# Sample attention with each key page on 32 partitions, turned by VectorE in 32 x 32 blocks, and scored by 32 x 32 tiles of TensorE

## The reference

```python
past_k = cache_fox_k[page_table].reshape(db, past_len, H_F, D_F)
past_v = cache_fox_v[page_table].reshape(db, past_len, H_F, D_F)
...
s = jnp.einsum('bqhd,bkhd->bhqk', qi, k, preferred_element_type=F32) * scale
s = s + ci.astype(F32).transpose(0, 2, 1)[..., None] - ckT
...
p = jax.nn.softmax(s, axis=-1)
return jnp.einsum('bhqk,bkhd->bqhd', p.astype(v.dtype), v)
...
mix = (g[:, :, 0] * ret_out + g[:, :, 1] * fox_out + g[:, :, 2] * mem_out) @ w_out
```

## Time and profile before

| | us |
|---|---|
| median of three runs | 3666.53 (3665.11 to 3673.05) |
| profiled execution, its own time | 3673.46 |
| its span, first to last instruction | 3671.6 |
| `phase_sample` in the span | about 2092 to 2616 |
| of it, 7 of the 8 sequences (56 of 64 quads) | 2130 to 2560 |

### The profile page before, as it was taken

The page is one execution under the profiler, slowest core; times in us unless marked ns, Lnnn a source line. Parts: engine busy times, 40 slices in busy tenths (PEclk is TensorE's granted clock), DMA queues, the critical chain, the costliest instruction groups (busy, mean ns, idle before and its releaser), DMA issues. The chain is left out here.

```text
span 3671.6 us, 56105 instructions
## 1 busy us (share of the span) xinstructions
PE 3314.7 (90%) x21121; PEld 2999.5 (82%) x21121; DVE 888.4 (24%) x1581; ACT 625.5 (17%) x1163; POOL 794.6 (22%) x696
## 2 busy tenths in 40 slices
PE   5999999997988898786799899999796999999996
PEld 5999999996887798554688666666686999999995
DVE  2111111114206211555101022222314111111114
ACT  3000000002101100344000144434203000000003
POOL 0232222323120131022111111111021223233220
PEclk8999999998997899899899999999798999999998
DMA  5111111111110112210211299999311111111111
GB/s 141 35 51 40 42 49 34 49 49 29 29 44 22 41 40 67 91 48 17 52 43 43 60 297 307 300 305 303 121 29 29 34 46 50 33 51 43 37 37 55
DMA packets 328667, 293.12 MB, mean 80 GB/s; under 512 B 33640, under 2 KB 249064, under 8 KB 328048
## 3 DMA queue, kind: packets, MB, share of 16 engines
q1 hardware_dynamic: 317136, 275.93, 24.3%
q0 software_dynamic: 11424, 15.76, 1.6%
HBM read 279.34 MB, written 12.26 MB: 79 GB/s over the span
## 5 line engine op out<-in xcount | busy, mean ns | idle before, releaser
L207 PE MATMUL f_acc<-x_hi,w_hi_last 128*128 128x364 f32 x1056 | 233.5, 329 | 27.5 <-SPq L489 27.5
L165 POOL CAST w_hi_first<-w_raw_first 128x1024 fp32r<-128x1024 f32 (+1 forms) x96 | 82.9, 863 | 738.4 <-issue 301.3
L207 PE MATMUL f_acc<-x_hi,w_hi_first 128*128 128x364 f32 x1056 | 233.5, 329 | 6.9 <-SPq L489 6.9
L207 PE MATMUL f_acc<-x_lo,w_hi_last 128*128 128x364 f32 x1056 | 234.0, 330 | 0.0
L207 PE MATMUL f_acc<-x_hi,w_lo_last 128*128 128x364 f32 x1056 | 234.0, 330 | 0.0
L207 PE MATMUL f_acc<-x_hi,w_lo_first 128*128 128x364 f32 x1056 | 233.9, 330 | 0.0
L207 PE MATMUL f_acc<-x_lo,w_hi_first 128*128 128x364 f32 x1056 | 233.7, 329 | 0.0
L207 PEld LDWEIGHTS f_acc<-x_hi,w_hi_last 128*128 128x128 f32 x1056 | 184.0, 189 | 28.0 <-issue 28.0
L165 POOL CAST w_hi_last<-w_raw_last 128x1024 fp32r<-128x1024 f32 (+2 forms) x92 | 73.5, 799 | 614.2 <-PE f_acc L207 610.2
L596 DVE SCALAR_TENSOR_TENSOR br<-f_acc,br 128x1092 f32 x88 | 114.1, 1296 | 368.8 <-PE f_acc L207 368.8
L207 PEld LDWEIGHTS f_acc<-x_hi,w_hi_first 128*128 128x128 f32 x1056 | 184.0, 189 | 7.1 <-issue 7.1
(11 more groups left out here) (399 smaller groups left out, 6321.8 us busy)
## 6 DMA issues: line engine op xcount, KB each, us to landing
br<-cache_fox_k SPq DMA_DIRECT2D x256, 256.0 KB, 5.6
br<-cache_fox_v SPq DMA_DIRECT2D x256, 256.0 KB, 6.5
w_raw_first<-w_ffn_gate SPq DMA_DIRECT2D x22, 512.0 KB, 3.8
w_raw_first<-w_ffn_up SPq DMA_DIRECT2D x22, 512.0 KB, 3.8
w_raw_last<-w_ffn_gate SPq DMA_DIRECT2D x22, 512.0 KB, 3.8
w_raw_last<-w_ffn_up SPq DMA_DIRECT2D x22, 512.0 KB, 3.8
w_raw_first<-w_ffn_down SPq DMA_DIRECT2D x40, 256.0 KB, 2.9
w_raw_last<-w_ffn_down SPq DMA_DIRECT2D x40, 256.0 KB, 2.8
```

The lines of the kernel that those rows point to most:

```text
L165: self.nc.gpsimd.tensor_copy(hi, raw).then_inc(self.high[s], 1)
L207: mm = self.nc.tensor.matmul(out[:, b, 0:width], w[s][:, k, :], x[:, k, b * width:(b + 1) * width], start=(k == 0 and first), stop=(k == k ...
```

## The change

Each key page is loaded onto 32 partitions (page x of a quad onto partitions 32x to 32x + 31, four tokens of 2 KB on each), by a DMA of its own as before. VectorE then turns blocks of 32 x 32 from `k_in` to `d_kt` in SBUF, two instructions of 128 x 1024 for a quad; TensorE's 16 transposes, the four ScalarE copies and their PSUM buffers are gone. The scores of a quad are 64 matmuls with 32 rows and 32 columns of the array and 128 columns of keys each, over all 16 positions of the array; each row group writes a PSUM bank of its own. The queries stand for this in `d_q_rep`, built by ScalarE for each sequence in 18 small copies, two in each step.

A score row is now a query of a head for all pages: the tile of a step is 128 x 512 (it was 128 x 256), there are four transposes of weights (two before), 16 products of 128 columns (8 of 256), and the exchange between pairs of rows is gone. ScalarE, no longer VectorE, copies the turned weights out. Scores, turned weights and products have one PSUM buffer each (two before). The filler is in all 9 steps, in blocks of 364, 364 and 296 + 64 tokens.

The bias ring now lies in `mem_kt` and `mem_v`. A slot holds two quads (four before), comes by 4 DMAs of 16 partitions, and there are 4 slots per sequence. The page table comes by one DMA (two before).

```diff
-        kt = [[g.mem_kt[:].rearrange("p a k -> p (a k)").rearrange("p (x c k) -> p x c k", x=2, c=PAIRS),
...
-        ring = [g.sb(ctx, f"d_ring{x}", [P, QUAD, 2, P]) for x in range(2)]
+        kt = [g.sb(ctx, f"d_kt{x}", [P, QUAD, H_F * DF]) for x in range(2)]
+        ring = [x[:].rearrange("p a k -> p (a k)").rearrange("p (m k) -> p m k", m=2) for x in (g.mem_kt, g.mem_v)]
...
+                def load_key(s, page):
+                    u, x = divmod(s, QUAD)
+                    sp.dma_start(k_in[ROWS * x:ROWS * (x + 1), u], keys[page].rearrange("(f t) h d -> t f (h d)", f=QUAD))\
+                        .then_inc(k_ok[s], 16)
...
                     for half in range(2):
+                        sp.wait_ge(k_turned, c * 4 + (2 * half + 2))
                         for s in range(half * QUAD, (half + 1) * QUAD):
-                            sp.wait_ge(k_turned, c * CH + (s + 1))
-                            sp.dma_start(k_in[:, s, :], keys[ahead[s]].rearrange("t h d -> t (h d)")).then_inc(k_ok[s], 16)
-                        sp.wait_ge(valued, c * 8 + (4 * half + 4))
+                            load_key(s, ahead[s])
+                        sp.wait_ge(valued, c * 2 + (half + 1))
...
+                def bias(slot):
+                    b, part = divmod(slot, QUAD)
+                    half, w = divmod(part, 2)
+                    if slot >= 2:
+                        pool.wait_ge(pturned, step_of(2 * (slot - 2) + 1) + 1)
...
                     if j > 0:
-                        pool.wait_ge(mixed, 2 * j)
+                        pool.wait_ge(mixed, 3 * j)
...
                 for b in range(NSEQ):
-                    more = b + 1 < NSEQ
-                    if more:
-                        bias(2 * b + 2)
+                    bias(4 * b + 2)
+                    bias(4 * b + 3)
+                    if b + 1 < NSEQ:
+                        bias(4 * b + 4)
                         weights(b + 1)
                         split(b + 1)
-                        bias(2 * b + 3)
+                        bias(4 * b + 5)
...
+                    for s in range(2):
+                        for h in range(2):
+                            for x in range(4):
+                                rows = slice(ROWS * x, ROWS * (x + 1))
+                                for c in range(PAIRS):
+                                    block = 4 * c + 2 * s + h
+                                    q = q_rep[e][rows, block * QW - s * LSEQ:block * QW - s * LSEQ + ROWS]
+                                    mm = nc.tensor.matmul(out[ROWS * c:ROWS * (c + 1), x], q,
+                                                          kt[u % 2][rows, :, block * ROWS:(block + 1) * ROWS],
...
+                def turn(u):
+                    for s in range(u % 2 * QUAD, (u % 2 + 1) * QUAD):
+                        dve.wait_ge(k_ok[s], 16 * (u // 2 + 1))
+                    if u >= 2:
+                        dve.wait_ge(scored, step_of(u - 2) + 1)
+                    for y in range(2):
+                        nc.vector.transpose(kt[u % 2][:, 2 * y:2 * y + 2, :], k_in[:, u % 2, 2 * y:2 * y + 2, :])\
+                            .then_inc(k_turned, 1)
...
                 for k in range(STEPS_ALL + 4):
-                    if 0 < k <= STEPS_ALL:
-                        place(k - 1)
...
-                    add_mix(k)
                     if k < STEPS_ALL:
                         top(k)
+                    u = quad_after(k)
+                    if u is not None:
+                        turn(u)
                     if 0 < k <= STEPS_ALL:
                         accumulate(k - 1)
                         if k % PIECES == 0:
-                            sums(k // PIECES - 1)
...
+                            finish(k // PIECES - 1)
+                    if k >= PIECES + 1 and (k - 1) % PIECES == 0:
+                        output((k - 1) // PIECES - 1)
+                    add_mix(k)
```

More of the change, by code:

```diff
@@ L302, in _ @@
                 sp.dma_start(g.b_forget[:], io["b_forget"].rearrange("(h o) -> h o", o=1)).then_inc(consts, 16)
[L303 to L306, removed]
+                sp.dma_start(g.pages[:], io["page_table"].rearrange("b n -> (b n)").unsqueeze(0)).then_inc(consts, 16)
                 sp.wait_ge(consts, 16 * n_const)
@@ L2465, in split @@
                     split_half(j, 1)
+                for e in range(2):
+                    nc.gpsimd.memset(q_rep[e][:], 0.0).then_inc(zeroed, 1)
+                    nc.gpsimd.memset(qz[e][:], 0.0).then_inc(zeroed, 1)
+                bias(0)
+                bias(1)
                 weights(0)
-                bias(0)
                 split(0)
-                bias(1)
                 for b in range(NSEQ):
-                    more = b + 1 < NSEQ
-                    if more:
-                        bias(2 * b + 2)
+                    bias(4 * b + 2)
+                    bias(4 * b + 3)
+                    if b + 1 < NSEQ:
+                        bias(4 * b + 4)
@@ L2498, in turn_probs @@
                     else:
-                        half, m = divmod(b * (PIECES - 1) + v - 1, QUAD)
-                        for x in range(2):
-                            mm = nc.tensor.transpose(ptp[:, k % 2, x, :], ring[half % 2][:, m, x, :], g.ident[:])
+                        slot, m = place_of(k)
+                        for y in range(QUAD):
+                            mm = nc.tensor.transpose(ptp[:, y, :], ring[slot % 2][:, m, y * P:(y + 1) * P], g.ident[:])
                     mm.then_inc(pturned, 1)
@@ new lines, in scores @@
+                    if k > 0:
+                        pe.wait_ge(topped, k)
+                    if k >= PIECES + 2 and v == 2:
+                        pe.wait_ge(out_ok, b)
+                    if v == 0:
+                        pe.wait_ge(q_ok, 18 * (b + 1))
+                        for c in range(PAIRS):
+                            mm = nc.tensor.matmul(stp[ROWS * c:ROWS * (c + 1), 0, 0:TS], qz[e][:, c, :], g.k_s[:, c, :],
+                                                  start=True, stop=True)
+                        mm.then_inc(scored, 1)
+                        return
@@ L2540, in swap_stats @@
-                def swap_stats(b):
-                    pe.wait_ge(summed, b + 1)
-                    if b == 0:
-                        pe.wait_ge(const, 32)
-                    nc.tensor.matmul(swapped, swap[:], stat[:, 0:2], start=True, stop=True).then_inc(swap_ok, 1)
+                    if k > 0:
+                        pe.wait_ge(acc_ok, k)
+                    for y in range(QUAD if v else 1):
+                        if v:
+                            n = u * QUAD + y
+                            pe.wait_ge(v_ok[n % CH], 16 * (n // CH + 1))
+                        for c in range(PAIRS):
+                            values = v_in[:, n % CH, c * P:(c + 1) * P] if v else g.v_s[0:TS, c * P:(c + 1) * P]
+                            mm = nc.tensor.matmul(ov[ROWS * c:ROWS * (c + 1), :],
+                                                  pt[0:P if v else TS, y, ROWS * c:ROWS * (c + 1)], values,
+                                                  start=(y == 0), stop=(y == QUAD - 1 or not v), skip_group_check=True)
@@ L2560, in gate_part @@
+                    nc.tensor.transpose(ot, on[:], g.ident[:]).then_inc(ot_ok, 1)
+                def gate_part(j, x, ks):
+                    if ks[0] == 0 and 4 * j + x > 0:
+                        pe.wait_ge(gated, 4 * j + x)
                     if x == 0:
@@ L2634, in exps @@
                     if v:
-                        half, m = divmod(b * (PIECES - 1) + v - 1, QUAD)
-                        probs = ring[half % 2][:, m].rearrange("p x k -> p (x k)")
+                        slot, m = place_of(k)
+                        probs = ring[slot % 2][:, m, :]
                     else:
```

359 lines of the change are left out of this document (145 added, 214 removed).

## The result

The changed kernel takes 3925.6 us (median of 4 runs, 3922.51 to 3926.85) against 3669.79 (4 runs, 3665.11 to 3677.57): a ratio of 1.069, 95% interval 1.0677 to 1.0702, or 256 us more. The forecast was 3780, slower, with a range to 3890: the sign was right, the loss more than twice the one forecast.

The account below looks back on a forecast made before the run. The prediction took DMA transfers as the bound, with TensorE close behind. Landing +95, bias on 16 partitions +6, late bias slot +14 and the dropped exchange -1.5 gave +113.5 us: 3780 us against the median, range 3655 to 3890.

Parts of the forecast that it names:

- I take 1.5, nearer the rows of the stage: Key loads onto 32 partitions cost the DMA engines 1.5 times as much: 37.4 us per sequence, +95 us in all.
- the `y_sample` pair: Output writes at the end: `y_sample` from 64 partitions 4.7 us per MB, `y_prompt` from 128 2.5, factor 1.9.
- the pair that I leaned on: GpSimd's queue in the stage: bias onto 32 partitions 4.0 us per MB, a weight tile onto 128 2.9, factor 1.39.
- the sum's own line: DMA time per sequence by landing factor: 1.5 gives 73.3 us (+95 in all), 1.9 gives 83.8 us (+179).
- That is below the DMA sum worked out next: TensorE's 43 to 65 us per sequence in the sample stage stays under the transfers' 69.7 us.
- The late bias slot: Top waits 9.8 us for bias at 7 block boundaries, mostly over transfers: 2 us net each, +14 us.
- The larger fear, +69: The seven 9.8 us waits for the bias slot with nothing hidden under transfers: +69 us.
- VectorE, the small matmuls: Per quad, two turnings 2.45 us (half to twice that) and score matmuls 1.0 to 3.8 us, hidden by transfers.
- C: VectorE's turning of 32 x 32 blocks costs four times the subtraction or more, +260 us: 3930; chance 0.04.
- D: The 64 small score matmuls don't overlap, TensorE 157 us per sequence: above 4400; chance 0.03.
- A: Narrow landing costs the DMA engines nothing and bias stalls are hidden: -20 to -29 us, about 3640; chance 0.13.
- B: Landing costs nothing, but the late bias slot is paid in part or full: 3667 to 3725; chance 0.14.

Follow-up runs that it names:

- e2: Changed kernel with GpSimd requesting the bias slot before the next block's filler weights, key pages still on 32 partitions: 3903.67 us (1.0648).
- e3: Changed kernel with both key pages on 128 partitions and the bias slot requested before the weights, output not the reference's: 3745.08 us (1.0182).
- e10: Kernel before with each key page landing on 32 neighbouring partitions and coarse waits for four pages, keys scrambled: 3850.71 us (1.0489).
- e11: Control: kernel before with only the coarse waits for four key pages, pages on 128 partitions: 3709.16 us (1.0111).
- e7: As e2, but each key page on 32 partitions spread over all 128 (x, x + 4, ...): 3773.97 us, one run.
- e8: As e2, but each key page on 64 neighbouring partitions, two tokens on each: 3893.29 us, one run.
- e16: Changed kernel with half the score instructions (32 matmuls of 256 columns per quad, scores not the reference's): 3910.30 us (1.0646).
- e5: As e3, but a quad's scores are 32 matmuls of 256 columns for 64 of 128, scores not the reference's: 3700.18 us (1.0064).
- e1: Changed kernel with each key page on 128 partitions again, late bias slot kept, output not the reference's: 3811.24 us (1.0383).
- e12: As e2, but a quad's four key pages requested in the order 0, 2, 1, 3: 3871.18 us, one run.
- e13: As e5, with finer refills: two key pages refilled after each turning, first turning waiting for two pages only: 3692.40 us (1.0047).
- e6: Kernel before with each score and product matmul of 256 columns cut into two of 128: 3682.34 us (1.0023).
- e9: As e4, with scores issued in 16 small groups between the filler's matmuls and VectorE and ScalarE reordered: 3834.68 us (1.0444).
- e4: As e3, with the top instruction split in four, one per page, so that the output is the reference's: 3740.46 us (1.0187).

## Why the prediction was wrong

**The landing: right mechanism, wrong size.** The step that failed is "I take 1.5, nearer the rows of the stage". e2 against e3 and e10 against e11 measure 1.9 for the keys. That was the factor of the `y_sample` pair, which I set aside as short and in the other direction. Why the pair that I leaned on the earlier trace rows shows less was not tested; my guess is that its bias came in between packets of pages on all partitions and saw only part of the crowding. With 1.9 the sum's own line gives +179 us for +95, and the whole sum 3864 us; the runs put the landing at 142 (e10 against e11) to 159 (e2 against e3). The rule of the Trainium skill that the prediction cited ("SBUF — State Buffer", "Door 1: The DMA port swizzle") goes by the ports that the partitions reach, and e7 and e8 agree with it; its figures (328 / 189 = 1.7) were nearer than my choice.

**TensorE's instructions: missing.** The second step that failed is "That is below the DMA sum worked out next". The prediction counted the columns of 64 small matmuls and put TensorE at 43 to 65 us per sequence; it never counted instructions. They are nearly three times as many per quad, cost nothing in its sum, and come in 16 KB pieces through the DMA engines that are 91% full. TensorE stops where such a piece has only just come: 119 us of "issue" waits of matmuls in 660 (82.9 + 25.0 + 9.2 + 1.5). In e3 its busy time of 7.2 us per quad and 1.4 us of such waits make 69 of the 72 us of a sequence; the DMA engines are busy for 62. The price depends on what bounds: 15 us with the narrow landing (e16 against the changed kernel), 45 without it (e5 against e3). So of the 62 us by which the changed kernel still exceeds the sum with 1.9 (3926 for 3864), the instructions explain 15 and the bias slot 8; the rest was not taken apart there.

**The late bias slot: right.** 15.4 us late each time in the waits (9.8 forecast), 22 us in all (14 forecast), because most of it lay under transfers, as argued. The larger fear, +69, is met only with wide pages, where the transfers don't bound: 66 us (e1 against e3), of some 100 that the top waits there.

**VectorE, the small matmuls: right.** 1.22 us per turning, 1.9 us for the scores (1.0 to 3.8 forecast); C and D are out, and so are A (the landing costs the DMA engines 1.9 times as much; in e12 neighbours on different halves give back 4 to 6%) and B, which had no cost of the landing.

**Signs that did not come.** The prediction listed a DMA share of 0.94 or more (it is 0.91), a turning that waits for key pages in most steps (4 waits, 10.3 us, in 55 quads), and keys that land later than values (7.7 us, values 11.1). TensorE's own stops and the bias stalls were where the engines waited instead.

In steps, from the changed kernel back: bias order 22, landing 159, half the score instructions 45, finer refills 8, and 18 that stay open (e13 to the kernel before): 252 of 256 us, the rest lying within what the medians of the kernel before differ by (3670 to 3675). The steps are not independent, since each uncovers the next. For the last 18, e13 shows TensorE waiting for value pages at a DMA share of 0.92 and 3.1 us per MB; whether the bias on 16 partitions, the single buffers or the pace of refills is behind it, no run told apart. The order matters too: taken the other way round, the wide landing alone is 114 (e1) and the bias order behind it 66.

## What to carry to other kernels

Before a tile is laid on a part of the partitions, take the DMA engines' time per MB from the queue rows of a narrow and a wide transfer, and use the worse pair; a stage that is 93% transfers pays most of the factor (142 to 159 us here, where 1.9 on the keys makes 179). Count instructions as well as columns when work is cut into small matmuls: a stage that saturates the DMA engines is the one that can least bring more code. And undo the parts in more than one order, because what a bound hides (instructions 15 us under it and 45 without, the late bias 22 and 66) shows only when the bound is gone.

## What was unexpected of the hardware

TensorE stops in the middle of unrolled code for 0.3 to 7.3 us and goes on 1.4 us (e3's median) behind the end of a 16 KB packet of the instruction queue, at some 360 records per quad of 9 to 12 us with the DMA engines 77% (e1) to 97% (e2) full; at 130 to 230 records per quad it hardly does (kernel before, e6, e5). Changing between 32 x 32 tiles and the whole array costs about 0.17 us each way (e9). The granted clock was 0.98 before, 0.77 after, and 0.85 in e3 with about 80% of the time busy. It does not follow the stops alone: e9, which waits 9 us for "issue", has 0.85 too, and e5, with 5 us, has 0.88, as e4 has with 69. How much of e3's loss is the clock and how much the stop itself was not tested.
